# The causal mask of an attention layer: matmuls on TensorE replaced by one addition on VectorE per head pair

## The reference

```python
scale = dh ** -0.5
l_own = jnp.einsum('bhcd,bhld->bhcl', qc, k_own).astype(jnp.float32) * scale
causal = (own * MOBA_BLOCK + pos_in_block)[None, :] <= qpos[:, None]
l_own = jnp.where(causal, l_own, -jnp.inf)
p = jax.nn.softmax(logits, axis=-1)
o = ... + jnp.einsum('bhcl,bhld->bhcd', p_own, v_own.astype(jnp.float32))
```

## Time and profile before

| | |
|---|---|
| median of three runs | 359.56 us (359.34 to 360.07) |
| the profiled execution's own time | 359.98 us |
| its span, first to last instruction | 358.2 us |
| TensorE matmul busy | 350.7 us, 98% |
| VectorE busy | 253.2 us, 71% |
| ScalarE busy | 184.5 us, 52% |
| GpSimd busy | 10.6 us, 3% |
| mean granted TensorE clock | 0.995 |

### The profile page before, as it was taken

How to read it: one execution, slowest core, us unless ns; L and a number is a source line. 1 busy time by engine, 2 the same in 40 slices (tenths; PEclk the granted TensorE clock), 3 DMA queues, 4 the chain that set the end, 5 groups by cost and what they waited for, 6 DMA issues and landing times.

```text
span 358.2 us, 4593 instructions
## 1 busy us (share of the span) xinstructions
PE 350.7 (98%) x1741; PEld 288.2 (80%) x1741; DVE 253.2 (71%) x305; ACT 184.5 (52%) x223; POOL 10.6 (3%) x18
## 2 busy tenths in 40 slices
PE   8999999999999999999999999999999999999993
PEld 4788888777778888888888888888888888888882
DVE  0969999999989589974757845639456394563734
ACT  3985663677796374535633635516355163551413
POOL 3000000000005000000000000000000000000000
PEclk9999999999999999999999999999999999999998
DMA  8998465533346463664455473853828547260003
GB/s 269 349 359 323 134 220 159 195 117 117 121 125 225 177 234 129 224 207 145 151 202 174 156 258 119 259 210 111 247 110 288 181 124 246 99 234 0 0 0 117
DMA packets 34089, 63.71 MB, mean 178 GB/s; under 512 B 1274, under 2 KB 5530, under 8 KB 34076
## 3 DMA queue, kind: packets, MB, share of 16 engines
q1 hardware_dynamic: 33588, 62.93, 51.9%
q10 hardware_dynamic: 488, 0.61, 0.5%
HBM read 62.48 MB, written 1.05 MB: 177 GB/s over the span
## 4 chain that ended last, share of the span: by engine, by line
PE 96%; issue 2%; ACT 1%; DVE 1%; POOLq 0%; POOL 0%; DVEq 0%; ACTq 0%
PE ps L874 20%; PE ps L876 20%; PE ps L875 20%; PE ps L1108 17%; PE ps L1110 8%; PE ps L861 4%; PE ps L968 1%; PE ps L900 1%; PE ps L920 1%; PE ps L921 1%; PE ps L927 1%; PE ps L996 1%; PE ps L971 0%; PE ps L1082 0%; ACT a_hi L419 0%
## 5 line engine op out<-in xcount | busy, mean ns | idle before, releaser
L874 PE MATMUL ps<-w_hi,a_lo 128*128 128x512 f32 x272 | 107.5, 395 | 0.0
L876 PE MATMUL ps<-w_lo,a_hi 128*128 128x512 f32 x272 | 106.1, 390 | 0.0
L875 PE MATMUL ps<-w_hi,a_hi 128*128 128x512 f32 x272 | 106.0, 390 | 0.0
L1108 PE MATMUL ps<-b_both,w_hi 128*128 128x512 f32 x256 | 90.8, 399 | 0.0
L1110 PE MATMUL ps<-b_both,w_lo 128*128 128x256 f32 x256 | 71.9, 281 | 0.0
L825 DVE TENSOR_TENSOR w_lo<-raw,w_hi 128x2048 fp32r<-128x2048 f32 x28 | 63.5, 2289 | 6.4 <-ACT w_hi L592 6.4
L399 ACT CAST w_hi<-raw 128x2048 fp32r<-128x2048 f32 (+1 forms) x30 | 53.8, 1799 | 20.7 <-PE ps L876 20.7
L618 DVE TENSOR_TENSOR w_lo<-raw,w_hi 128x2048 fp32r<-128x2048 f32 x26 | 59.3, 2286 | 3.2 <-ACT w_hi L399 3.2
L874 PEld LDWEIGHTS ps<-w_hi,a_lo 128*128 128x128 f32 x272 | 51.1, 188 | 11.0 <-issue 0.5
L876 PEld LDWEIGHTS ps<-w_lo,a_hi 128*128 128x128 f32 x272 | 51.0, 188 | 11.0
L875 PEld LDWEIGHTS ps<-w_hi,a_hi 128*128 128x128 f32 x272 | 51.1, 188 | 10.0
(11 more groups left out here) (122 smaller groups left out, 258.5 us busy)
## 6 DMA issues: line engine op xcount, KB each, us to landing
raw<-in_w_ff_dram SPq DMA_DIRECT2D x32, 1024.0 KB, 5.6
raw<-in_w_in_dram SPq DMA_DIRECT2D x14, 1024.0 KB, 5.3
raw<-in_w_in_dram SPq DMA_DIRECT2D x16, 256.0 KB, 6.7
raw<-in_w_out_dram SPq DMA_DIRECT2D x4, 1024.0 KB, 5.0
raw<-in_w_attn_up_dram SPq DMA_DIRECT2D x2, 1024.0 KB, 4.9
raw<-in_w_conv_pw_dram SPq DMA_DIRECT2D x2, 1024.0 KB, 5.3
res<-in_x_dram SPq DMA_DIRECT2D x2, 512.0 KB, 3.8
gfin_bc<-in_g_final_dram SPq DMA_DIRECT2D x1, 512.0 KB, 7.0
```

What stands on the lines that cost most here:

```text
L874: nc.tensor.matmul(dst, lo[:, tok], w_hi[:, slot, k], start=start, stop=False)
L875: nc.tensor.matmul(dst, hi[:, tok], w_hi[:, slot, k], start=False, stop=False)
L876: return nc.tensor.matmul(dst, hi[:, tok], w_lo[:, slot, k], start=False, stop=stop)
L1108: nc.tensor.matmul(ps[:, TB + c], w_hi[:, slot, k, cols], b_both[:, kk].rearrange("p a t -> p (a t)"), start=kk == 0, stop=False)
```

## The change

The mask becomes a float32 tile `mask` of 128 x 2 x 128, one triangle for each query tile. `scores(p)` keeps its four matmuls in the source (eight instructions in the trace) and loses the four that add the mask. `row_max(p)` begins with one VectorE addition over both heads' banks, columns 128 to 383, which are the two diagonal blocks, in place; it waits for that addition's own completion (`masked`) and goes on as before. On GpSimd the zeroed tile, the selection and the copy of the identity to bf16 become one zeroed tile and one selection; TensorE's wait for the third of these goes.

```diff
-        ident_b = sb("ident_b", [P, P], BF16)
-        mask_b = sb("mask_b", [P, T], BF16)
+        mask = sb("mask", [P, TT, P])
@@ gpsimd
-            nc.gpsimd.memset(mask_b[:], 0.0).then_inc(const_made, 1)
+            nc.gpsimd.memset(mask[:], 0.0).then_inc(const_made, 1)
-            nc.gpsimd.affine_select(out=mask_b[:], in_=mask_b[:], compare_op=ALU.is_ge, fill=MASKED, base=P,
-                                    pattern=[[-1, T]], channel_multiplier=1).then_inc(ident_made, 1)
+            nc.gpsimd.affine_select(out=mask[:], in_=mask[:], compare_op=ALU.is_ge, fill=MASKED, base=0,
+                                    pattern=[[0, TT], [-1, P]], channel_multiplier=1).then_inc(mask_made, 1)
-            nc.gpsimd.tensor_copy(ident_b[:], ident[:]).then_inc(ident_made, 1)
@@ vector
             def row_max(p):
                 dve.wait_ge(scored, p + 1)
+                dve.wait_ge(mask_made, 1)
+                diagonals = ps[:, SB0:SB0 + 2, P:3 * P]
+                nc.vector.tensor_tensor(diagonals, diagonals, mask[:].rearrange("p (h s) k -> p h (s k)", h=1).to_broadcast([P, 2, 2 * P]),
+                                        ALU.add).then_inc(masked, 1)
+                dve.wait_ge(masked, p + 1)
                 nc.vector.tensor_reduce(smax[:, p, 0:2], ps[:, SB0:SB0 + 2, 0:256], AX.X,
@@ tensor
                     for h in range(2):
                         rows = slice(HD * h, HD * h + HD)
-                        nc.tensor.matmul(ps[:, SB0 + h, at:at + keys], qk_t[rows, 0, p, s * P:s * P + P],
-                                         qk_t[rows, 1, p, 0:keys], start=True, stop=False)
-                    for h in range(2):
-                        last = nc.tensor.matmul(ps[:, SB0 + h, at + keys - P:at + keys], ident_b[:], mask_b[:, P:T],
-                                                start=False, stop=True)
+                        last = nc.tensor.matmul(ps[:, SB0 + h, at:at + keys], qk_t[rows, 0, p, s * P:s * P + P],
+                                                qk_t[rows, 1, p, 0:keys], start=True, stop=True)
                 last.then_inc(scored, 1)
@@
                     if n == S_ATT:
                         pe.wait_ge(qk_made, 2)
-                        pe.wait_ge(ident_made, 3)
```

More of the change, by code:

```diff
@@ L252, in build @@
         qk_made = sem("qk_made")
+        mask_made = sem("mask_made")
         scored = sem("scored")
+        masked = sem("masked")
         max_made = sem("max_made")
```

## The result

The changed kernel takes 362.12 us, the median of six runs (361.66 to 362.57), against 359.56 for the kernel before (359.34 to 360.07): a ratio of 1.0066, 95% interval 1.0056 to 1.0076. It is 2.6 us slower, where 2.56 was forecast.

A forecast was written before the change was run, and what follows sets the result against it. TensorE, busy 98%, was taken as the bound, with a VectorE-ScalarE chain level at unit 14. Four additions of 0.72 us less 0.32 make 2.56; 359.56 + 2.56 = 362.1 us, range 361.1 to 364.0.

The forecast's parts named there:

- the tie: At the head of unit 14, ScalarE's gates were level with TensorE, with no slack; the wait there was 0.2 us.
- the chain: From 69.56 to unit 14, four row maxima on VectorE, then ScalarE, then TensorE, claimed unbroken.
- The addition's price: On VectorE ahead of each pair's row maximum: 0.72 us per addition, four in all, bounds 0.61 and 0.79.
- The earlier start: At VectorE's first maximum: the addition starts at 69.24 in place of 69.56, 0.32 us won once.
- The delay at pair 3: Pair 3's `nbias`, `low` and reciprocal on VectorE come 4 x 0.72 - 0.32 = 2.56 us later.
- TensorE's saving: 16 mask matmuls fewer on TensorE: 0.32 us a pair, 1.3 in all; with gaps at most 0.58 a pair, 2.3.
- the first rival: At the head of unit 14: VectorE's additions are covered and only TensorE's saving counts, 358.3 us; chance 4%.
- The second: At pair 3 and unit 14: only the transposes count and the gates don't, 361.1 us; chance 6%.
- The third: On VectorE or ScalarE: some 2 us of slack hidden by the merged timeline, result about 359.9 us; chance 4%.
- The fourth: On TensorE from unit 14: its clock falls after the stalls, some 2 us more, 364.1 us; chance 10%.
- The fifth: On VectorE: each addition is dearer than any row, at 1.0 us, giving 363.3 us; chance 8%.

The follow-up runs named there:

- the control: The kernel before with 12 convolution products moved on VectorE from steps 9 to 11 to step 12, mask matmuls kept: 359.94 us, ratio 1.0004.
- 12 products later: Two kernels, the changed one and the one before, each with 12 convolution products moved from steps 9 to 11 to step 12: 357.53 us and 359.94 us.
- masks on both engines: The kernel before with its mask matmuls kept and the VectorE mask addition put in as well: 362.21 us, ratio 1.0069.
- six products earlier: The kernel before with 6 convolution products brought forward on VectorE from step 13 to steps 9 to 11: 362.25 us, ratio 1.0052.
- mask on neither: The changed kernel without the VectorE addition, so with no causal mask at all: 359.07 us, ratio 0.9977.
- the dose: The changed kernel with 6 convolution products moved on VectorE from steps 9 to 11 to step 12: 359.89 us, ratio 0.9995.

## Why the prediction was right

**The bound and the tie.** That ScalarE's gates stood level with unit 14 was read from one wait of 0.2 us and two rows 0.06 us apart. The kernel with six products brought forward shows the tie directly: 2.4 us put on VectorE there arrive on TensorE as 2.3. Since the control is unchanged at 33.72 us, VectorE's part in the tie cost the kernel before nothing.

**One reading of the chain was off, by 0.07 us.** The prediction let the chain of before run unbroken from VectorE's first maximum at 69.56 into the reciprocal. But the reciprocal starts 97.02 - 94.75 = 2.27 us after its `low` there and 2.20 after it in the changed kernel (98.92 - 96.72), so in the kernel before it waited 0.07 us, too little for a bracket. It waited for ScalarE's sums, whose exponentials stood behind two copies that TensorE's value matmuls of pair 1 (at 93.38) had released:

```profile
94.30 0.37 ACT L488 COPY o_t<-ps 128x256 f32<-128x256 f32 x1 [1.99 <-PE ps L996]
94.56 0.81 ACT L495 COPY probs_t<-ps 128x768 f32<-128x768 f32 x1
```

Two paths were thus level at pair 3, one from TensorE over ScalarE and one of VectorE with 0.07 us to spare. The first explains why unit 14 still waits its 0.2 us in both kernels with 12 products later: from the value matmuls of pair 1 to unit 14 it is 7.98 us before, and 7.98 and 7.99 in those two. The spare time shows in every run whose stage VectorE sets: how much later than before its last `low` comes in the stage, less 0.07, is what the stage grows by, to 0.02 us. The two are 2.58 and 2.50 for the change, 2.92 and 2.84 with masks on both engines, 0.20 and 0.11 for six products later, 2.37 and 2.29 for six products earlier, and -0.35 and -0.43 with mask on neither. The mechanism forecast holds; that this slack was 0.07 us and not 1 was not established ahead of the result, and here the forecast had some luck.

**The addition's price** was taken as 0.72 us from the earlier trace rows and measured 0.72 to 0.73, with a duration of 0.69 or 0.70. The write into PSUM, for which there was no row, costs nothing that can be seen. The Trainium skill (VectorE: DVE Perf Modes, on the TRN2 errata) would have had 0.065 us more for the PSUM source; the trace doesn't agree: 0.69 to 0.70 us with source and output in PSUM, 0.69 with all in SBUF.

**The earlier start** of the first row maximum was given as 0.32 us, with VectorE's own convolution products as what is late next. The addition does start at 68.62, 0.10 us ahead of the products' end at 65.06 + 3.66 = 68.72. The run without any mask shows the gain alone: 0.43 us of stage, and the difference between the additions with and without mask matmuls is 36.55 - 36.21 = 0.34. The first of these is 0.35 us of an earlier start and the 0.07 above.

**The delay at pair 3.** Its `low` was forecast 2.56 us later than 94.75; it starts at 96.72, 1.97 later in a profile that is 0.61 early (67.65 - 67.04): 2.58. Unit 14 comes 2.50 us later in the stage, by the 0.07 above.

**One term was mis-sized, without effect on the sum: TensorE's saving.** I took what the mask matmuls hold the engine for, 0.32 us a pair, and kept 0.58 as the upper bound. From the scores to the next unit it was 69.34 - 67.97 = 1.37 us (the first from the earlier trace rows, the second from the row of before shown with the result); it is 68.21 - 67.36 = 0.85 now. That is 0.52 us a pair, 2.08 in all and not 1.28. So the gaps around the short bf16 matmuls went with them: the score matmuls alone held TensorE for (68.60 - 67.97) + (69.24 - 68.82) = 1.05 us between them, and hold it for 0.85 now. As the chain swallows all of it, it only made the stalls longer: saving and loss make 2.08 + 2.50 = 4.6 us, where 3.84 was forecast. The four brackets shown add up to 4.06, without the gaps that stand there anyway. It would have mattered in the first rival, whose price should have been 357.5 and not 358.3, and it did in the kernel that beats both.

**The rivals.** The first (only the saving counts) came true as soon as the chain was relieved, at 357.53 us, and was decided by VectorE as the forecast said. The second (gates off the chain, 361.1) is out: unit 14's own wait of 0.90 us is in the trace. The third (hidden slack of 2 us) is out by the dose, where each 0.40 us on VectorE is 0.40 us on TensorE; the slack was 0.07. The fourth: the granted clock stays at 1.00 (2.4 GHz) through the stalls of 1.5 and 0.9 us, and the matmuls behind them start 0.33 and 0.23 us apart (103.25, 103.58, 103.81), as in the kernel before (101.36, 101.69, 101.93). The changed kernel in three stretches, PEclk behind the POOL column:

```profile
95.00:100.00 5.00, 4.16 (x19) 3.09 (x17) 4.93 (x9) 2.59 (x11) 0.00 (x0) 1.00 0.00 0
100.00:104.00 4.00, 2.43 (x17) 1.80 (x18) 3.81 (x10) 3.97 (x7) 0.00 (x0) 1.00 0.84 268
104.00:110.00 6.00, 6.00 (x31) 4.51 (x30) 4.98 (x9) 6.00 (x8) 0.06 (x1) 1.00 0.16 56
```

The distances settle it better than the column does, which reads 1.00 also over the start of the kernel before:

```profile
1.00:5.00 4.00, 3.80 (x9) 1.19 (x9) 0.14 (x1) 1.49 (x2) 2.34 (x8) 1.00 0.80 272
```

There the warm-up matmuls take 0.45 us each. So that these ran at the lower level, on which the prediction's price for this rival rests, no granted clock in the profile shows.

The fifth (a dearer addition) is out by its 0.69 us.

## What to carry to other kernels

Work that is taken off the busiest engine is worth nothing while another engine's chain stands level with it; before moving work, find the smallest wait of the bound engine and follow it back, since the queue you want to load may be that chain, whatever its mean load. Here a queue with 71% load was full for 28 us on end but for 0.07 us, and 12 operations with a later deadline stood in it ahead of the urgent ones: moving them behind, one line, turned a loss of 2.6 us into a gain of 2.2 (1.8 to 3.1 by the ratio). And when an edit fails, test it together with what relieves the chain: neither of the two edits was worth anything without the other.

## What the runs showed of the hardware that I had not expected

Short bf16 matmuls between the float32 score matmuls cost more than the time they hold TensorE. Four mask matmuls a pair were to be read as 0.32 us, and 0.52 us went with them. Whether the type, or the change between 64 and 128 rows, makes the gaps, no run here tells apart.

GpSimd and VectorE seem to hold each other up. In the kernel before, one convolution product out of 120 takes 2.61 us in place of 0.48, and ends at 113.72, 0.3 us behind GpSimd's one long operation. Before, VectorE and GpSimd:

```profile
108.07 5.37 POOL L381 TENSOR_TENSOR bias_rows<-gfin_bc,bias_rows 1x1024 fp32r<-1x1024 f32 x1 [89.42 <-ACT bias_rows L525]
108.91 2.28 DVE L618 TENSOR_TENSOR w_lo<-raw,w_hi 128x2048 fp32r<-128x2048 f32 x1
111.11 2.61 DVE L672 SCALAR_TENSOR_TENSOR conv<-z,dw,conv 128x256 f32<-128x256 f32 x1
```

In the changed kernel with the 12 products moved, GpSimd's operation starts 0.8 us ahead of the end of a `low` and runs on beside the nine products behind it:

```profile
104.86 2.29 DVE L618 TENSOR_TENSOR w_lo<-raw,w_hi 128x2048 fp32r<-128x2048 f32 x1
106.32 3.09 POOL L381 TENSOR_TENSOR bias_rows<-gfin_bc,bias_rows 1x1024 fp32r<-1x1024 f32 x1 [86.50 <-ACT bias_rows L525]
107.07 5.80 DVE L672 SCALAR_TENSOR_TENSOR conv<-z,dw,conv 128x256 f32<-128x256 f32 x9
```

VectorE's nine products take 5.80 us in place of 3.64: again one of them is 2.1 us too long. In every kernel here one product, and only one, is that long. In both of these GpSimd's operation ends 2.25 or 2.26 us behind the end of the `low` that it meets, whenever it started, and so it does in five more of the eight kernels, with 3.08 to 6.47 us for the same operation. With masks on both engines it meets no `low` and takes 2.40 us, the shortest. The Trainium skill (SBUF — State Buffer, who interferes with whom) describes a port pair that the two engines share and that one of them holds for a whole instruction; the wait behind `low` and the held product fit that. It doesn't say why GpSimd, in the kernel before, was also kept waiting through the end of the products ahead of that `low` (108.07 to 108.91). No run here took the GpSimd operation away, so it is an explanation and not shown. It cost no time in any of these kernels, but with VectorE's reserve at step 16 now used up it may in the next.
